# Last product of a two-layer block: 64 of 192 dense tokens moved from split fp32r products to plain fp32 products in the array's column halves

## What is computed

```
def _peer(h, w_query, sub_keys, expert_u, expert_v):
    ...                                    # 8 heads, top 16 of 16384 experts each: 128 choices per token
    def block(args):
        xt, it, gt = args
        u = expert_u[it]
        act = jax.nn.gelu(jnp.einsum('td,tkd->tk', xt, u))
        return jnp.einsum('tk,tkd->td', gt * act, expert_v[it])
...
x = x + _peer(_rmsnorm(x, norm_ffn[l]), ...)
return _rmsnorm(x, norm_final)
```

## Time and profile before

| what | value |
|---|---|
| time, median of 2 runs | 1615.19 us (1614.3 to 1616.08) |
| time of the profiled execution | 1615.85 us |
| its span on the core | 1614.2 us |
| mean granted TensorE clock over the span | 0.996 |
| PE busy | 1537.5 us (95%), 9505 instructions |
| DVE / ACT / POOL busy | 944.0 / 686.7 / 556.7 us |
| last product, first matmul to the last tile's first | 1312.9 to 1599.5 us |

### The profile page before, as it was taken

One profiled execution on the slowest core, in us unless ns is written; L12 is line 12 of the kernel. 1 busy time (PEld: TensorE's weight loads), 2 busy tenths in 40 slices (PEclk: granted clock), 3 DMA queues, 4 the chain that ended last, 5 costly groups with the idle time before them and its releaser, 6 DMA issues.

```text
span 1614.2 us, 23533 instructions
## 1 busy us (share of the span) xinstructions
PE 1537.5 (95%) x9505; PEld 1212.7 (75%) x9505; DVE 944.0 (58%) x1600; ACT 686.7 (43%) x1032; POOL 556.7 (34%) x323
## 2 busy tenths in 40 slices
PE   8999999999889888999999999999999999999998
PEld 6889654434334333888989999999999998888886
DVE  5876422101101110776554688778777879988987
ACT  6665411101001000665452444344488865555554
POOL 4111100000000000422131443343488776878872
PEclk9999999999999999999999999999999999999999
DMA  8435999999999999635344455555544479999994
GB/s 296 156 107 188 422 400 421 421 421 421 421 421 421 421 421 410 237 132 173 128 157 157 139 195 194 169 195 194 191 143 139 131 278 329 362 360 346 367 363 175
DMA packets 99345, 444.82 MB, mean 276 GB/s; under 512 B 11152, under 2 KB 19856, under 8 KB 57632
## 3 DMA queue, kind: packets, MB, share of 16 engines
q1 hardware_dynamic: 86256, 404.90, 66.4%
q0 software_dynamic: 11264, 33.60, 5.8%
q10 hardware_dynamic: 1712, 4.76, 0.8%
HBM read 435.26 MB, written 7.86 MB: 275 GB/s over the span
## 4 chain that ended last, share of the span: by engine, by line
PE 61%; DMA 22%; DVE 7%; POOL 4%; ACT 3%; issue 3%; ACTq 0%; SPq 0%; DVEq 0%
DMA big<-in_w_up 12%; PE ps L503 11%; PE ps L504 11%; PE ps L505 11%; PE ps L700 8%; PE ps L1205 6%; PE ps L1197 4%; DMA fix<-in_w_up 3%; DMA hh<-in_w_up 3%; PE ps L1149 3%; DMA big<-in_expert_v,tig 2%; POOL big L2642 2%; POOL small L2673 2%; DVE fix_parts L1248 1%; ACT fix_parts L2142 1%
## 5 line engine op out<-in xcount | busy, mean ns | idle before, releaser
L2619 POOL TENSOR_TENSOR fix_parts<-fix,fix_parts 128x512 fp32r<-128x512 f32 x59 | 129.9, 2202 | 672.1 <-ACT fix_parts L2142 672.1
L505 PE MATMUL ps<-hh_parts,fix_parts 128*128 128x256 f32 x1120 | 317.3, 283 | 0.0
L700 PE MATMUL ps<-big 128*64 128x512 f32 x800 | 249.0, 595 | 17.9 <-DMA big<-in_w_up 9.3
L503 PE MATMUL ps<-hh_parts,fix_parts 128*128 128x256 f32 x768 | 219.9, 286 | 6.4 <-issue 5.6
L504 PE MATMUL ps<-hl_parts,fix_parts 128*128 128x256 f32 x768 | 217.9, 284 | 0.0
L505 PEld LDWEIGHTS ps<-hh_parts,fix_parts 128*128 128x128 f32 x1120 | 215.2, 192 | 0.0
L1248 DVE TENSOR_TENSOR fix_parts<-fix,fix_parts 128x1536 fp32r<-128x1536 f32 (+1 forms) x84 | 173.0, 2060 | 62.7 <-ACT fix_parts L2142 60.4
L700 PE MATMUL ps<-fix,big 128*64 128x512 f32 x528 | 189.4, 594 | 17.5 <-DMA big<-in_w_up 9.1
L2142 ACT ACTIVATE fix_parts<-fix 128x2048 fp32r<-128x2048 f32 x84 | 160.8, 1916 | 65.6 <-PE ps L1205 48.1
L700 PEld LDWEIGHTS ps<-big 128*64 128x64 f32 x800 | 79.8, 137 | 110.8 <-issue 109.9
L503 PEld LDWEIGHTS ps<-hh_parts,fix_parts 128*128 128x128 f32 x768 | 147.7, 192 | 7.7 <-issue 7.6
(11 more groups left out here) (420 smaller groups left out, 3661.8 us busy)
## 6 DMA issues: line engine op xcount, KB each, us to landing
fix<-in_expert_u SPq DMA_DIRECT2D x64, 1024.0 KB
fix<-in_expert_v SPq DMA_DIRECT2D x38, 1024.0 KB
big<-in_w_up SPq DMA_DIRECT2D x34, 1024.0 KB, 26.5
big<-in_w_down SPq DMA_DIRECT2D x34, 1024.0 KB, 25.5
big<-in_w_gate SPq DMA_DIRECT2D x32, 1024.0 KB, 26.4
big<-in_expert_v SPq DMA_DIRECT2D x26, 1024.0 KB
fix<-in_w_gate SPq DMA_DIRECT2D x23, 1024.0 KB, 26.0
fix<-in_w_up SPq DMA_DIRECT2D x22, 1024.0 KB, 26.6
```

What stands on the lines that cost most here:

```text
L503: pe.matmul(o, l[0], r[0], start=first, stop=False)
L505: return pe.matmul(o, l[1], r[0], start=False, stop=last)
L700: ins = pe.matmul(m.PS[64 * i:64 * i + 64, bank, :], lhs(h * k_of // 2 + k, i), view(t.place[t.slot[x]])[:, k, c0:c0 + 512], start=(h + k ...
L2619: nc.gpsimd.tensor_tensor(m.fr(x[:, at:2048]), x[:, at:2048], m.fr(hi[:, at:2048]).bitcast(F32), ALU.subtract).then_inc(s.lo_g, 1)
```

## The change

1. `first_block` is gone. `first_tokens(i)` takes its place: 4 plain fp32 matmuls with 64-column weights read straight from `m.W` and the raw `expert_v` tile. Block j goes to column half j, so partitions 0 to 63 of banks 2 and 3 collect the blocks j = 0 and 64 to 127 the blocks j = 1. `joint` folds them as before.
2. `first_tokens(i + 1)` is issued ahead of tile i's 12 split matmuls (`others(i)`), since it needs the raw tile, which DVE's low half overwrites. It waits for the tile's landing and signals `raw`; `dve_low` of an `expert_v` tile waits for that signal.
3. `w_high` and `w_low` handle only the last 128 dense tokens: ACT's copy goes from 384 to 256 elements per partition, and of DVE's two subtractions only the one of 256 is left.
4. At tile 0, `first_tokens(0)` and `first_tokens(1)` stand in a row, the eight early products are gone, and DVE's `dve_low` of tile 0 moves behind `weigh_acts(62)`.
5. The signals `fold` and `parts` are one; ACT's copy of banks 2 and 3 waits for `raw` 64 in place of `half`.

```
-        def first_block():
-            for j in range(2):
-                for half in range(2):
-                    for y in range(2):
-                        ins = pe.matmul(m.PS[:, 2 + half, :], both[:, j, 0:P], v[y][:, 1024 * j + 512 * half:1024 * j + 512 * half + 512], ...)
...
+    def first_tokens(i):
+        tile = f["expert_v"] + i
+        v = t.place[t.slot[tile]]
+        pe.wait_ge(s.land[t.landing[tile]], 16 * t.turn[tile])
+        if i >= MAPS_AT:
+            pe.wait_ge(s.early, i - MAPS_AT + 1)
+        for half in range(2):
+            for j in range(2):
+                ins = pe.matmul(m.PS[64 * j:64 * j + 64, 2 + half, :], m.W[:, 2 * i + j, 0:64],
+                                v[:, 1024 * j + 512 * half:1024 * j + 512 * half + 512],
+                                start=(i == 0), stop=(i == 63), skip_group_check=True)
+        ins.then_inc(s.raw, 1)
...
+    pe.wait_ge(s.weighed, DENSE // 4)
+    first_tokens(0)
+    for i in range(64):
+        if i < 63:
+            first_tokens(i + 1)
+        pe.wait_ge(s.lo_v, t.split[f["expert_v"] + i] + 1)
         pe.wait_ge(s.w_lo, i + 1)
-        ins = first_block()
...
+        if i < 63:
+            others(i, (0, 1)).then_inc(s.used, 2)
+        else:
+            others(i, (0,)).then_inc(s.used, 1)
             joint()
+            others(i, (1,)).then_inc(s.used, 1)
...
     nc.vector.wait_ge(s.hi, n + 1)
+    raw = t.tile_of[n] - t.first["expert_v"] + 1
+    if raw > 0:
+        nc.vector.wait_ge(s.raw, raw)
...
-        ve.tensor_tensor(lo_first, w[:, :, 0:64], hi[:, :, 0:64], ALU.subtract)
-        ve.tensor_tensor(lo, w[:, :, 64:DENSE], hi[:, :, 64:DENSE], ALU.subtract).then_inc(s.w_lo, 1)
+        ve.tensor_tensor(lo, w[:, :, 64:DENSE], hi.bitcast(F32), ALU.subtract).then_inc(s.w_lo, 1)
...
-    ac.wait_ge(s.half, 1)
+    ac.wait_ge(s.raw, 64)
     ac.wait_ge(s.summed, SPARSE)
```

More of the change, by code:

```diff
@@ L179, in signals @@
     s.picked = [one(f"acts_picked{i}") for i in range(4)]
-    s.summed, s.fold, s.half, s.parts, s.joint = one("row_summed"), one("fold"), one("half_out"), one("part_sums"), one("joint")
+    s.summed, s.raw, s.parts, s.joint = one("row_summed"), one("raw_used"), one("part_sums_and_fold"), one("joint")
     s.w_hi, s.w_lo, s.y_sq, s.y_out = one("w_hi"), one("w_lo"), one("y_sums"), one("y_out")
@@ L346, in buffers @@
     m.gf = EB[1][:, 0:1024]
-    m.WP = [DS[:, 0:768], yf[:, 0:768], yf[:, 768:1536]]
+    m.WP = [DS[:, 0:512], yf[:, 0:512], yf[:, 768:1280]]
     m.F = EB[1][:, 1024:1088]
@@ L489, in w_blocks @@
     both = m.fr(m.WP[i % 3]).rearrange("p (j c) -> p j c", j=2)
-    return both[:, :, 0:64], both[:, :, 64:64 + DENSE], both[:, :, 64 + DENSE:2 * DENSE]
+    return both[:, :, 0:P], both[:, :, P:2 * P]
 def blocks_before(u):
@@ L1178, in joint @@
     def joint():
-        pe.wait_ge(s.fold, 1)
-        pe.wait_ge(s.parts, 2)
+        pe.wait_ge(s.parts, 3)
         for half in range(2):
@@ L1186, in joint, with others @@
         ins.then_inc(s.joint, 1)
-    for i in range(64):
+    def first_tokens(i):
[10 more added lines that the diff above has]
+        ins.then_inc(s.raw, 1)
+    def others(i, halves, passes=((0, 0), (0, 1), (1, 0))):
         n = t.split[f["expert_v"] + i]
@@ L1191, in tensor_second @@
         both = m.fr(m.WP[i % 3]).rearrange("p (j c) -> p j c", j=2)
-        def first_block():
+        for half in halves:
             for j in range(2):
-                for half in range(2):
-                    for y in range(2):
[L1197 to L1202, removed]
-                for j in range(2):
[L1204 to L1212, removed]
+                for x, y in passes:
+                    ins = pe.matmul(m.PS[:, half, :], both[:, j, P * x:P * x + P], v[y][:, 1024 * j + 512 * half:1024 * j + 512 * half + 512],
+                                    start=(i + j + x + y == 0), stop=(i == 63 and j + x == 2), skip_group_check=True)
+        return ins
+    pe.wait_ge(s.weighed, DENSE // 4)
[4 more added lines that the diff above has]
+        pe.wait_ge(s.lo_v, t.split[f["expert_v"] + i] + 1)
         pe.wait_ge(s.w_lo, i + 1)
-        ins = first_block()
-        if i == 63:
-            ins.then_inc(s.half, 1)
-            second_block((0,), ((0, 0), (0, 1), (1, 0))).then_inc(s.used, 1)
+        if i < 63:
+            others(i, (0, 1)).then_inc(s.used, 2)
+        else:
+            others(i, (0,)).then_inc(s.used, 1)
             joint()
-            second_block((1,), ((0, 0), (0, 1), (1, 0))).then_inc(s.used, 1)
-        else:
-            second_block((0, 1), ((1, 0),) if i == 0 else ((0, 0), (0, 1), (1, 0))).then_inc(s.used, 2)
+            others(i, (1,)).then_inc(s.used, 1)
 def share_of(t, n):
@@ L1957, in w_low @@
         w = m.W[:, 2 * i:2 * i + 2, :]
-        lo_first, hi, lo = w_blocks(m, i)
-        hi = hi.bitcast(F32)
+        hi, lo = w_blocks(m, i)
         ve.wait_ge(s.w_hi, i + 1)
-        ve.tensor_tensor(lo_first, w[:, :, 0:64], hi[:, :, 0:64], ALU.subtract)
-        ve.tensor_tensor(lo, w[:, :, 64:DENSE], hi[:, :, 64:DENSE], ALU.subtract).then_inc(s.w_lo, 1)
+        ve.tensor_tensor(lo, w[:, :, 64:DENSE], hi.bitcast(F32), ALU.subtract).then_inc(s.w_lo, 1)
     dve_low(nc, m, s, t, first)
@@ L1969, in vector_second @@
             weigh(q)
-        dve_low(nc, m, s, t, first + i + 1)
+        if i < 63:
+            dve_low(nc, m, s, t, first + i + 1)
         if i > MAPS_AT:
             weigh_acts(i - 1)
+        if i == 63:
+            dve_low(nc, m, s, t, first + 64)
         for what, b, n in ROUTING.get(i, ()):
@@ L1997, in vector_second @@
     ve.wait_ge(s.used, t.used[f["expert_v"] - 1])
-    ve.tensor_tensor(m.F, m.ident[:, 0:64], m.ident[:, 64:128], ALU.add).then_inc(s.fold, 1)
+    ve.tensor_tensor(m.F, m.ident[:, 0:64], m.ident[:, 64:128], ALU.add).then_inc(s.parts, 1)
     at = 0
@@ L2556, in w_high @@
             ac.wait_ge(s.used, t.used[f["expert_v"] + i - 3])
-        ac.activation(w_blocks(m, i)[1], m.W[:, 2 * i:2 * i + 2, :], ACT.Copy).then_inc(s.w_hi, 1)
+        ac.activation(w_blocks(m, i)[0], m.W[:, 2 * i:2 * i + 2, 64:DENSE], ACT.Copy).then_inc(s.w_hi, 1)
     for i in range(64):
```

## The result

The changed kernel takes 1636.31 us (median of 2 runs, 1635.67 to 1636.94) against 1615.19 us before: a ratio of 1.0123, 95% interval 1.0096 to 1.0151. Its profiled execution took 1635.67 us, with a span of 1634.1 us. So the change costs 21 us, where 18 were forecast.

What follows compares the result with a forecast made beforehand. PE was taken to bound the last product. Form changes +16.9, stall -1.0, start +1.2 and end +1.2 us gave +18.3 on 1615.85 us, 1634.2; less 0.66 for the median, 1633.5 us, bounds 1627 to 1643 us.

Steps and rivals of the forecast that it cites:

- The bound: Last product: PE sets the time, busy 285.99 of 286.60 us, with DVE close behind at 89%.
- The halves: Plain fp32 matmuls in the two column halves run side by side, 0.856 us per pair, 1.71 us for four.
- The serial rival: Last product: the column halves run one after another, +1.71 us per tile, about 1743 us; chance 0.03.
- The change of form: Each tile: going from 128-column to 64-column weights and back makes a tile +0.27 us; +16.9 us over all tiles.
- the rival at 1610 us: Last product: weight loads run under the running matmul, so the change of form is hidden and only streaming counts; chance 0.07.
- The gap of 0.10 us ahead of the joint: Ahead of the joint: wait for ACT's copy or change of form; price 2.08 us if form, 1.98 if wait.
- The four plain matmuls: Each tile: four plain matmuls cost 2.08 us in place, 1.71 of it streaming, against 1.81 us removed; turn 4.80 us.
- The start: Start of the last product: PE waits for DVE's split of tile 0 and `w_low`, +1.2 us.
- The end: Ahead of the joint: PE waits for DVE's copy after the last row sum, +1.2 us.
- DVE's wait: Steady turns: `dve_low` waits for `first_tokens`, with 1.8 us to spare, so no stall; row sums' waits shrink.
- the stall in the middle: Last product: PE's single wait of 1.0 us for DVE goes with the slower turn, -1.0 us.
- The rival's mechanism: A turn with two row sums plus a row wait over 1.5 us stalls PE; +10 to +15 us, 1644 to 1649 us; chance 0.13.

Runs made afterwards that it cites:

- two tiles in a row: Changed kernel with the plain products of two tiles, then the split products of two, halving the changes of form: 1622.74 us, ratio 1.0041.
- the two ends changed: Changed kernel with the last row sum one turn earlier and tile 0's plain products in the middle of the last `expert_u` tile: 1635.16 us, ratio 1.0112.
- all-plain run: Changed kernel with all 192 dense tokens as plain fp32 in the column halves and the `expert_v` split copies left out: 1652.45 us, ratio 1.023.
- the run with 128 columns: Changed kernel with a tile's four plain fp32 matmuls given 128-column weights over all 128 partitions instead of 64-column halves: 1720.09 us, ratio 1.0648.
- half and twice the changes: Changed kernel with plain products of two tiles grouped (half, 1622.74 us), or each turn's four plain matmuls cut into two separate pairs (twice, 1659.17 us).
- three tiles in a row: Changed kernel with the plain products of three tiles in a row, then the split products of three: 1650.98 us, ratio 1.0212.

## Why the prediction was right

**The bound.** PE set the time before and does after: it is busy for all of the 62 turns. The run without row sums shows that DVE's row sums, POOL and the row fetches are no second bound. DVE is not far, though. With two tiles in a row and with the two ends changed, single turns had PE waiting for DVE, 0.5 to 1.2 us each.

**The halves.** They run side by side at 0.856 us per pair, as read from line 700; 0.858 in the all-plain run. The serial rival is out: a turn would have been 6.2 us and more.

**The change of form.** It is real and not hidden (the rival at 1610 us is out), and it comes with the change of columns: the run with 128 columns shows that the types alone cost nothing, the all-plain run that the halves alone cost nothing, and half and twice the changes that it counts by the change. The gap of 0.10 us ahead of the joint, which the prediction left open between a wait and the form, is the form: the same 0.09 us stands ahead of every `first_tokens` without a wait. The rule of the Trainium skill ("TensorEngine Tiling (Array Packing)", Key Properties), that a change of tiling mode drains the engine, agrees.

**The term that was mis-sized.** The four plain matmuls were priced at 2.08 us from the joint, with the second split matmul behind it as the end of the sum. The prediction made a turn 4.80 us of this; it is 4.85. Last start ahead to second start behind is about 2.53 us in the changed kernel too, as forecast. The missing 0.05 us lies in the ten steps behind that point, 2.33 instead of 2.27 us, most of it in the first four, 0.24 instead of 0.2265 us. They could have been read before: behind the joint the trace of the kernel before has starts at 1604.98, 1605.22, 1605.46 and 1605.69 us, and I stopped at the first of them. The prediction's own row from the experts had it too: it gives six matmuls in 1.51 us instead of 1.36, 0.15 us too long, and the sum took only the 0.11 of the first step. 62 x 0.05 = 3.1 us.

**The start.** Timeline of DVE and PE after, against the earlier trace rows:

```profile
1311.67 3.65 PE L1196 MATMUL ps<-big 128*64 128x512 f32 x16
...
1313.72 2.29 DVE L1252 TENSOR_TENSOR big_parts<-big,fix_parts 128x2048 fp32r<-128x2048 f32 x1 [6.22 <-PE ps L1196]
1315.93 0.42 DVE L1964 TENSOR_TENSOR big_parts<-big,big_parts 128x256 fp32r<-128x256 f32 x1
...
1316.50 0.47 PE L1209 MATMUL ps<-fix_parts,big_parts 128*128 128x512 f32 x1 [1.18 <-DVE big_parts L1964]
...
1319.07 0.39 PE L1209 MATMUL ps<-fix_parts,big_parts 128*128 128x512 f32 x1
```

Forecast +1.2 us, measured 1.18.

**The end.** Against the earlier trace rows:

```profile
1620.28 1.63 PE L1209 MATMUL ps<-fix_parts,big_parts 128*128 128x512 f32 x6
1621.36 1.22 DVE L2012 COPY big<-ps 128x1024 f32<-128x1024 f32 x1
...
1622.64 1.94 PE L1183 MATMUL ps<-big,hl 128*64 128x512 f32 x8 [0.74 <-DVE big L2012]
```

The copy ends at 1622.58 and the joint starts 0.06 us later, not 0.22. The 0.22 us taken from before were mostly the engine finishing its own row, and not the signal. The joint was also due later than forecast. With T at 1617.2 us, it was due at T + 4.6 (1620.28 + 1.63 - 0.39 + 0.32 = 1621.84) and not T + 4.4, since the split matmuls ahead were slower. The two make the stall 0.8 us instead of 1.2.

**DVE's wait.** No stall of PE in 62 turns; the row waits shrank as said, and the stall in the middle went (its 1.0 us is idle time of the weight loads; PE's own starts lost about 0.85 us there). The rival's mechanism is real even so: with a row wait of 2.78 us in the run on the two ends, a stall of 1.18 us reached PE. In the changed kernel the longest row wait was 1.9 us.

**The sum again.** Against the forecast the form change cost 3.1 us more and the end 0.4 us less. 62 x (4.852 - 4.532) = 19.8, tiles 0 and 1 about +0.2, start +1.2, end +0.8, the old stall -1.0: +21.0 us. The spans say the same: from the last product's first matmul to the end there are 1634.1 - 1311.67 = 322.4 us after and 1614.2 - 1312.93 = 301.3 us before, +21.1. (The profiled times differ by only 19.8 us, since the unchanged part ahead ended 1.3 us earlier in the profiled execution of the changed kernel.)

## What to carry to other kernels

Using the array in column halves saves passes, but each trip there and back costs about 0.4 us on TensorE, some 1.8 fp32r matmuls of 512 columns; so count trips before passes. Here a trip per tile bought 0.10 us of streaming, and would need some four tiles per trip to pay (0.4 / 0.10, an estimate from the turns above). With five landing slots three tiles per trip already cost more than two. Price such a trip from a place where one already stands in a running row, and follow the steps behind it until they are back at their usual distance.

## What the runs showed that I had not expected

- After a change from 64 to 128 columns, not only the first step is longer (0.34 us): the ten behind it take 2.33 us instead of 2.27. With the row sums gone the twelve still take 3.06 us, so the row sums, POOL and the row fetches don't cause it. Nor is it the change of columns alone. Behind the wait at the start of the changed kernel, twelve split matmuls start within 2.57 us (1316.50 to 1319.07), the first step 0.31 us and the ten others at 0.2265. And in the kernel before, where matmuls of 256 columns go over to such of 512 without a change of weight columns, the first seven steps take 1.61 us (1312.93 to 1314.54) instead of 1.585. What does cause it is open.
- A wait of PE can cost more than its length. In the run with three tiles in a row the granted clock was 0.50 behind a wait of 3.57 us, and the plain matmuls there took 3.68 us in place of 1.94.
- Going between fp32r and fp32 at 128 columns costs at most 0.02 us per turn, for both ways together.
- Plain fp32 for all 192 tokens, with ACT idle and DVE doing row sums only, is just 2.3% slower than the split kernel: 1652.45 against 1615.0 us.
